# Gate logits over four column groups, joined log-forget sums and earlier value parts in a two-block kernel

## The reference, cut to what matters

```
sh1, sc1, ... = split(silu(c) @ ada_w + ada_b, 6)            # and the same for c_ctx
hx = rmsnorm(x, pre_mix_g) * (1 + sc1) + sh1                 # hc likewise, from ctx
p  = h @ m_in_w + m_in_b                                     # for hx and for hc
q, k, v, o, gates = split(p, [512, 1024, 2048, 3072])        # gates: 16 columns
logi_fwd, f_fwd, logi_bwd, f_bwd = gates as 4 x 4 heads
logf = log_sigmoid(f)                                        # per token, head and direction
b    = cumsum(logf)                                          # per chunk of 128 tokens ...
...                                                          # ... forward, and reversed
m, decay weights, scores * exp(b_t - b_s + logi_s - m_t), states from the context, outputs
```

## Time and profile before

| what | value |
|---|---|
| median of three runs | 819.86 us |
| lowest and highest | 817.09 and 819.89 us |
| span of the profiled execution | 815.9 us |
| the three runs, less this span | 1.2, 4.0 and 4.0 us |
| TensorE products busy | 780.6 us, 96% |
| weight loads, VectorE, ScalarE, GpSimd | 82%, 66%, 51%, 11% |
| mean granted TensorE clock | 0.993 |
| HBM | 177 GB/s over the span |

### The profile page before, as it was taken

How to read it: one execution, slowest core, us unless ns; L and a number is a source line. 1 busy time by engine, 2 the same in 40 slices (tenths; PEclk the granted TensorE clock), 3 DMA queues, 4 the chain that set the end, 5 groups by cost and what they waited for, 6 DMA issues and landing times. The chain is left out here.

```text
span 815.9 us, 11773 instructions
## 1 busy us (share of the span) xinstructions
PE 780.6 (96%) x4599; PEld 669.7 (82%) x4599; DVE 540.0 (66%) x714; ACT 414.7 (51%) x582; POOL 92.5 (11%) x150
## 2 busy tenths in 40 slices
PE   4899999999999999999989999999999999999996
PEld 3777787777789898988789998988888998988884
DVE  0673789977588778887478786654466666654465
ACT  2623413453676776644266555556364545543264
POOL 4000130401100000000060313210100000000000
PEclk9999999999999999999999999999999999999998
DMA  9963667732456556669536342321465655545611
GB/s 309 361 242 119 217 241 254 277 131 91 129 189 199 168 191 206 206 219 322 182 82 206 104 156 54 105 102 52 153 205 185 206 170 190 192 155 194 226 59 51
DMA packets 107900, 144.83 MB, mean 178 GB/s; under 512 B 6343, under 2 KB 70352, under 8 KB 107856
## 3 DMA queue, kind: packets, MB, share of 16 engines
q1 hardware_dynamic: 100512, 137.38, 50.7%
q10 hardware_dynamic: 7280, 6.83, 2.7%
q0 software_dynamic: 64, 0.01, 0.0%
HBM read 142.10 MB, written 2.10 MB: 177 GB/s over the span
## 5 line engine op out<-in xcount | busy, mean ns | idle before, releaser
L2074 PE MATMUL ps<-h_parts,w_hi 128*128 128x512 f32 x504 | 179.6, 396 | 0.0
L1276 DVE TENSOR_TENSOR w_lo<-raw,w_hi 128x2048 fp32r<-128x2048 f32 (+1 forms) x61 | 135.6, 2230 | 63.9 <-ACT w_hi L666 63.7
L666 ACT CAST w_hi<-raw 128x2048 fp32r<-128x2048 f32 (+1 forms) x61 | 112.9, 1852 | 78.2 <-PE ps L1950 56.6
L2073 PE MATMUL ps<-h_parts,w_lo 128*128 128x256 f32 x504 | 140.5, 279 | 0.0
L1284 DVE TENSOR_TENSOR w_lo<-raw,w_hi 128x2048 fp32r<-128x2048 f32 x44 | 100.7, 2289 | 16.2 <-ACT w_hi L674 15.7
L2074 PEld LDWEIGHTS ps<-h_parts,w_hi 128*128 128x128 f32 x504 | 94.6, 188 | 19.5
L2073 PEld LDWEIGHTS ps<-h_parts,w_lo 128*128 128x128 f32 x504 | 95.0, 188 | 3.3
L674 ACT CAST w_hi<-raw 128x2048 fp32r<-128x2048 f32 x44 | 84.0, 1908 | 0.0
L1948 PE MATMUL ps<-w_hi,act_hi 128*128 128x512 f32 x176 | 69.0, 392 | 0.0
L1950 PE MATMUL ps<-w_hi,act_lo 128*128 128x512 f32 x176 | 68.5, 389 | 0.0
L1949 PE MATMUL ps<-w_lo,act_hi 128*128 128x512 f32 x176 | 68.5, 389 | 0.0
(11 more groups left out here) (419 smaller groups left out, 1557.4 us busy)
## 6 DMA issues: line engine op xcount, KB each, us to landing
raw<-in_ffn_up_w SPq DMA_DIRECT2D x22, 1024.0 KB, 5.0
raw<-in_w_gate_up SPq DMA_DIRECT2D x22, 1024.0 KB, 5.0
raw<-in_ada_w SPq DMA_DIRECT2D x16, 1024.0 KB, 5.2
raw<-in_w_in SPq DMA_DIRECT2D x14, 1024.0 KB, 5.2
raw<-in_m_in_w SPq DMA_DIRECT2D x11, 1024.0 KB, 5.2
raw<-in_ffn_down_w SPq DMA_DIRECT2D x10, 1024.0 KB, 5.3
raw<-in_w_down SPq DMA_DIRECT2D x10, 1024.0 KB, 5.0
raw<-in_m_out_w SPq DMA_DIRECT2D x4, 1024.0 KB, 5.0
```

The costliest lines, as they stand in the source:

```text
L666: act.copy(part_view(w_hi, s), raw_view(split[s])).then_inc(hi_ready, 1)
L1276: dve.tensor_tensor(part_view(w_lo, s), raw_view(split[s]), part_view(w_hi, s).bitcast(F32), ALU.subtract).then_inc(lo_ready, 1)
L2073: pe.matmul(both[:, 0], lo[:, k, w], h_hi[:, k, :], start=False, stop=False)
L2074: ins = pe.matmul(both, hi[:, k, w], h_parts[:, :, k, :], start=False, stop=k == KD - 1)
```

## The change

The gates of block one are computed in another form. TensorE multiplies the fp32 gate weights (`wg`, now 32 columns wide of which 16 are zero) by the fp32 streams `full` and `cfull`: sixteen fp32 products instead of 32 in parts, each feature tile in one of four column groups, so that four partial sums stand in rows 0, 32, 64 and 96 of bank 4. `gate_rows` and `fold` have 128 rows instead of 32, and `fold` adds the four partial sums (and still the rows 0 and 16, for block two, which keeps its form). The gate weights' high and low part of block one are no longer made. `wg` moves into a part of the buffer `r4`; GpSimd zeroes its second half and makes `fold` behind the first norm's scales. The accumulators of the late modulation exchange places, since `full` must last until the gates are made. The sums of log-forget values take both token tiles in one product of eight columns, with one correction of four columns each. `hi_until(5)` moves from behind the softplus to before the copy of the gate rows, and `lo_until(5)` from behind the sums to before the wait for the gates by token.

```diff
-        gate_rows = sb(ctx, "gate_rows", [32, 2 * T])
+        gate_rows = sb(ctx, "gate_rows", [P, 2 * T])
-        fold = sb(ctx, "fold", [32, 16])
+        fold = sb(ctx, "fold", [P, 16])
...
-            ada_acc = (acc1[:, 0], acc1[:, 1], acc2[:, 0], acc2[:, 1])
+            ada_acc = (acc2[:, 0], acc2[:, 1], acc1[:, 0], acc1[:, 1])
...
-                wg = sb(mx, "wg", [P, KD, 16])
+                wg = r4[:, MH * P:MH * P + 32 * KD].rearrange("p (k n) -> p k n", k=KD)
...
@@ GpSimd
-            link(pool.memset(fold[:], 0.0))
-            for part in range(2):
-                link(keep(fold[:], ALU.not_equal, [[-1, 16]], 1, fill=1.0, base=-16 * part))
...
+            link(pool.memset(fold[:], 0.0))
+            for row in (0, 16, 32, 64, 96):
+                link(keep(fold[:], ALU.not_equal, [[-1, 16]], 1, fill=1.0, base=-row))
+            pool.memset(wg[:, :, 16:], 0.0).then_inc(S("const_ready"), 1)
@@ ScalarE
-            load(wg[:], I["m_in_w"][0][:, gate0:gate0 + 16].rearrange("(k p) n -> p k n", p=P), "wg_in")
+            load(wg[:, :, 0:16], I["m_in_w"][0][:, gate0:gate0 + 16].rearrange("(k p) n -> p k n", p=P), "wg_in")
...
-            act.wait_ge(S("wg_in"), 32)
-            act.copy(wg_parts[:, :, 0:16], wg[:]).then_inc(S("wg_hi"), 1)
-
-            def gate_rows_out(i, n):
+            def gate_rows_out(i, rows, n):
                 act.wait_ge(S("gate_rows_mm"), i)
-                act.copy(gate_rows[:, 0:n], ps[0:32, 4, 0:n]).then_inc(S("gate_rows"), 1)
+                act.copy(gate_rows[0:rows, 0:n], ps[0:rows, 4, 0:n]).then_inc(S("gate_rows"), 1)
...
-            hi_until(4)
-            gate_rows_out(1, 2 * T)
+            hi_until(5)
+            gate_rows_out(1, P, 2 * T)
...
             act.activation(sp1[:], sp1[:], ACT.Ln, bias=ones[:, 0:1]).then_inc(S("softplus"), 1)
-            hi_until(5)
...
-            gate_rows_out(2, T)
+            gate_rows_out(2, 32, T)
@@ VectorE
             lo_x(0)
-            gate_weights_lo(1, wg)
...
             ada2_group()
+            lo_until(5)
             dve.wait_ge(S("gate_mm"), 1)
...
             dve.tensor_copy(b_ctx[:], ps[0:MH, 4, 32:34]).then_inc(S("u_ready"), 1)
-            lo_until(5)
@@ TensorE
+            def gates_by_group():
+
+                pe.wait_ge(S("wg_in"), 32)
+                pe.wait_ge(S("const_ready"), 3)
+                for c, stream in enumerate((full, cfull)):
+                    for half in range(2):
+                        for kk in range(4):
+                            k = 4 * half + kk
+                            ins = pe.matmul(ps[32 * kk:32 * kk + 32, 4, c * T:(c + 1) * T], wg[:, k, :], stream[:, k, :],
+                                            start=half == 0, stop=half == 1)
                 ins.then_inc(S("gate_rows_mm"), 1)
...
-                    ins = pe.matmul(ps[:, 4, 16 * t:16 * t + 16], gate_rows[:, t * P:(t + 1) * P], fold[:], start=True, stop=True)
+                    ins = pe.matmul(ps[:, 4, 16 * t:16 * t + 16], gate_rows[0:rows, t * P:(t + 1) * P], fold[0:rows], start=True,
+                                    stop=True)
...
-            gates_by_row(1, ((h_hi, h_lo), (c_hi, c_lo)))
+            gates_by_group()
             keys_c(3).then_inc(group_used, 1)
-            gates_by_token(1, 2 * TT, "gate_mm")
+            gates_by_token(1, 2 * TT, P, "gate_mm")
...
             for a in range(2):
-                for t in range(TT):
-                    for d in range(2):
-                        dst = ps[:, 4, 16 * a + 8 * t + 4 * d:16 * a + 8 * t + 4 * d + 4]
-                        tri = ((s_le_t, s_ge_t), (s_gt_t, s_lt_t))[a][d]
-                        other = t != (a + d) % 2
-                        pe.matmul(dst, tri[:], lf_of(TT * a + t, d), start=True, stop=not other)
-                        if other:
-                            pe.matmul(dst, ones[:], lf_of(TT * a + 1 - t, d), start=False, stop=True)
+                sums = ps[:, 4, 16 * a:16 * a + 16].rearrange("p (t d h) -> p d t h", t=TT, d=2)
+                gates = lf[:, 2 * TT * a:2 * TT * (a + 1), :].rearrange("p (t d) h -> p d t h", d=2)
+                for d in range(2):
+                    tri = ((s_le_t, s_ge_t), (s_gt_t, s_lt_t))[a][d]
+                    t = 1 - (a + d) % 2
+                    pe.matmul(sums[:, d], tri[:], gates[:, d], start=True, stop=False)
+                    pe.matmul(sums[:, d, t, :], ones[:], lf_of(TT * a + 1 - t, d), start=False, stop=True)
```

More of the change, by code:

```diff
@@ L1351, in _, with gate_weights_lo @@
             dve.tensor_copy(cols[:], ps[:, 7, 2 * KD:2 * KD + n_col]).then_inc(S("vec_T"), 1)
-            def gate_weights_lo(i, src):
-                dve.wait_ge(S("wg_hi"), i)
+            def gate_weights_lo(src):
+                dve.wait_ge(S("wg_hi"), 1)
                 lo_part(wg_parts[:, :, 16:], src[:], wg_parts[:, :, 0:16], "wg_lo")
@@ L1675, in gdn @@
                 lo_until(at["gdn"][j] + 4)
-            gate_weights_lo(2, wsm)
+            gate_weights_lo(wsm)
             gdn(0)
@@ L2177, in _, with gates_by_row, gates_by_token @@
             first_transposed(0, 3)
[L2179 to L2187, removed]
-                ins.then_inc(S("gate_rows_mm"), 1)
-            def gates_by_token(i, tiles, want):
+            def gates_by_group():
[7 more added lines that the diff above has]
+                                            start=half == 0, stop=half == 1)
+                ins.then_inc(S("gate_rows_mm"), 1)
+            def gates_by_row(parts):
+                pe.wait_ge(S("wg_lo"), 1)
+                for k in range(KD):
+                    for part in parts:
+                        ins = pe.matmul(ps[0:32, 4, 0:T], wg_parts[:, k, :], part[:, k, :], start=k == 0 and part is parts[0],
+                                        stop=k == KD - 1 and part is parts[1])
+                ins.then_inc(S("gate_rows_mm"), 1)
+            def gates_by_token(i, tiles, rows, want):
                 pe.wait_ge(S("gate_rows"), i)
                 for t in range(tiles):
-                    ins = pe.matmul(ps[:, 4, 16 * t:16 * t + 16], gate_rows[:, t * P:(t + 1) * P], fold[:], start=True, stop=True)
+                    ins = pe.matmul(ps[:, 4, 16 * t:16 * t + 16], gate_rows[0:rows, t * P:(t + 1) * P], fold[0:rows], start=True,
+                                    stop=True)
                 ins.then_inc(S(want), 1)
@@ L2513, in _ @@
             gdn_tiles(0)
-            gates_by_row(2, ((h_hi, h_lo),))
-            gdn_tiles(1, between=lambda: gates_by_token(2, TT, "gate_mm"))
+            gates_by_row((h_hi, h_lo))
+            gdn_tiles(1, between=lambda: gates_by_token(2, TT, 32, "gate_mm"))
             gdn_tiles(2)
```

## The result

| | before | changed |
|---|---|---|
| median of four runs | 819.12 us | 810.14 us |
| lowest to highest | 817.09 to 819.89 | 808.05 to 812.09 |
| span of the profiled execution | 815.9 us | 809.1 us |
| TensorE products busy | 780.6 us | 776.0 us |
| stretches at 0.50 of TensorE's clock between 20 us and the last products | 2 | 1 |

The ratio is 0.9904, 95% interval 0.9883 to 0.9925: faster by 0.8 to 1.2%, against 813.4 us forecast within 810.0 to 816.3. The spans differ by 6.8 us, the first medians by 9.0. In three later series, with 27, 11 and 11 runs of the kernel before, its median was 817.3 to 817.5, and the changed kernel, timed again, had 810.4. One run each of experiments 1 and 4 took 2.73 ms: both count in the medians given there and not in the ratios.

The account below looks back on a forecast made before the run. TensorE, busy 780.6 of 815.9 us, was taken to bound the kernel. Savings 0.2 + 1.6 + 0.9 + 2.06 + 1.7 = 6.5 us from the median 819.86 gave 813.4 us, range 810.0 to 816.3.

Parts of the forecast that it names:

- Start: At the kernel's start, dropping ScalarE's cast of the gate weights brings L800, which TensorE awaits, earlier: 0.2 us saved.
- Gates: Block one's gates from 61.70 us: sixteen fp32 products in four column groups take 2.06 instead of 3.68 us, 1.6 saved.
- Gates by token: Four products behind the gates, now 128 rows instead of 32; duration goes by columns, so 0 (bounds -0.1 and +0.3).
- Sums: Sums from 73.42 us: joining both tiles leaves 16 instructions instead of 24 at 0.111 us each, 0.9 us saved.
- The wait: TensorE's idle time before the first value product at 82.48 us goes, as value parts are made earlier: 2.06 us saved.
- The second fall: Clock at 0.50 from 83.9 to 87.3 us, behind the idle stretch, goes with it: 1.7 us saved.
- Does it last?: Behind the value block, later chains and waits move along, so the 6.5 us saving stays to the end.
- One rival: Column groups run in turn: gates 7.4 instead of 3.7 us, total gain 0.7, 819.2 us; 0.04 including gain lost otherwise.
- The likeliest case, one fall left: The clock's fall behind the sums stays and the second goes: 6 to 7 us gained, chance 0.52.
- no fall: Rival: the shorter sums no longer let the clock fall either; 8.2 us gained, 811.7 us, chance 0.18.

Follow-up runs that it names:

- experiment 1: Kernel before with only the gates over four column groups; sums per tile and late value parts kept: median 817.91 us, ratio 0.9989.
- experiment 4: Changed kernel with the value group's high and low parts put back behind the softplus and the sums: median 815.11 us, ratio 0.9976.
- experiment 3: Kernel before with only the value group's high and low parts made before the gates: median 813.59 us, ratio 0.9937.
- experiment 7: Changed kernel with all sixteen fp32 gate products in one column group, gate rows copied as 32 rows: timed once, 815.64 us.
- experiment 6: The changed kernel repeated without edits, as control: 810.40 us, ratio 0.9907.
- experiment 10: Changed kernel with early identity products while TensorE waits for the first weights, and the sums in two pieces with full products between: 808.68 us, ratio 0.9881.
- experiment 11: Changed kernel with the sums in two pieces and full products between, run again: 810.28 us, ratio 0.9913.
- experiment 5: Changed kernel with the first query tile's last products put between the two halves of the sums: 809.88 us, ratio 0.9904.

## Why the prediction was right

Span against span the forecast was 6.5 us, and 6.8 was measured: the mechanism was right, and the sizes nearly. The time itself, 810.14 us, lies only 0.14 us inside the range and outside the 812 to 814.5 that the prediction called its own; that it fell inside at all is in part luck, as the paragraph behind the terms shows. Term by term, changed against before:

- *Start, 0.2.* TensorE's wait for L800 is 1.28 instead of 1.48 us in every kernel without the cast: 0.20. Here the two executions differed by 0.07 at that point, since transfers and the clock's first rise scatter more than this.
- *Gates, 1.6.* 1.87 instead of 3.68, with 0.10 lost going in (60.74 to 61.74 is 1.00 us for the four last keys) and 0.10 coming out (0.50 instead of 0.40): 1.6. The form was in the trace already, and that made the term exact.
- *Gates by token, forecast 0.* Measured 0.18 gained in the step (66.47 to 67.28 is 0.81; before 68.22 to 69.21 us it was 0.99) and about 0.08 ahead of it. I had said that duration goes by columns; it doesn't quite.
- *Sums, 0.9.* 2.94 to 2.04: 0.90, and 0.83 when alone. The spacing of the trace held. By the 60 cycles of the Trainium skill ("TensorEngine Tiling (Array Packing)", Instruction Overhead) the prediction had an estimated 0.2 us, which would have missed four fifths of it. What a tiny product costs here is most likely the load of its weights: weight loads are busy for 2.93 of 3.00 us, and the last eight instructions, whose weights have 4 columns instead of 128, take 0.27 us together against 0.11 us each. No run varied this alone.
- *The wait, 2.06.* From the sums' end to the value product 3.89 instead of 6.12 us: 2.23, 0.17 more than the idle 2.06. The idle time is counted from the end of the last turn, 0.42 us behind its start, but without a wait the value product starts 0.03 us behind that start: 0.39 us more. Against this the clock falls earlier, 0.3 instead of 0.7 us behind the sums' end, and the work up to the last turn takes 0.21 us longer. VectorE's slack was forecast at 1.7 and is 1.63.
- *The second fall, 1.7.* The rest is 731.67 instead of 733.39: 1.72. Experiments 3 and 4 tie it to the idle time: 1.59 and 1.78.
- *Does it last?* 731.67 us of rest also in experiment 7, which reaches the value block 4.5 us later: the 730 us behind are rigid but for the clock.

The sum is 0.07 + 4.99 + 1.72 = 6.8. One rival had its price slightly wrong: gates of 7.4 us with 0.2 us for the column groups leave 0.9 us of gain, not 0.7; experiment 7 lost 5.48 us up to the value block, which leaves 1.3. The likeliest case, one fall left, is what both profiles of the changed kernel have at this place. The timed median came out lower than the forecast, 810.1 against 813.4, because I took 819.86, the median of three, as the base; with 817.4, as the later series have it, the same saving gives 810.9. I had put 1.2 to 4.0 us around the span of the profiled execution; the runs show 1.7 to 1.8, so its own time was 817.6, and 2.3 us of the base belonged to slower executions. Of the 49 later runs of the kernel before, 10 took 819.7 us or more, as two of my three did. Taking the saving from one execution and the base from another was the weak step, without a reason given. The low end of the range, put there for a faster base together with no fall, caught it.

## What to carry to other kernels

Look for a wait whose releasing engine sat idle shortly before, with its data already landed: moving that work in the written order was the part of this change that gained most, and it added no instruction. Count what an idle stretch or a run of tiny products does to TensorE's clock behind it, and break such a run with full products where other work is ready (here 1.5 us in the traces, not clear of the scatter in the timed runs). And judge microseconds between fixed points of the trace: two executions of one kernel differed by 2.4 us in span, more than any single term of this change.

## What the runs showed of the hardware that I had not expected

- *The rate at the start is not in the granted clock.* The rows before the clock's first rise (16.7 to 24.8 us) carry a clock of 1.00 on the page, but the same sixteen instructions last 1.94 us at 9.6 us and 1.07 later. The durations tell, not the column.
- *Fewer rows of the stationary operand cost a little more.* The turns of gate rows take 0.81 us with 128 rows and 0.99 with 32 (experiment 7), and the four full products ahead of them 0.92 against 1.00. The Trainium skill ("TensorEngine Tiling (Array Packing)", Key Properties) says that a change of the array's mode drains it; the two crossings in experiment 7, 0.26 us for 32 rows, fit that.
- *Falls far away.* At 407 to 415 us a fall comes in some executions (experiments 1, 4, 6, 10 and 11) and not in others, behind the same idle 2.36 us. So an idle time of over 2 us brought a fall in 5 of 13 profiles there, while the idle 2.0 us before the value block had one behind it in all three kernels that have it (before, 2 and 4). In experiments 6 and 11, where it is the only fall behind the value block, the rest is longer: by 1.1 us than in the changed kernel's first profile, by 0.4 us than in experiment 5.
